# Two rotations between reciprocal and rescaling, the key tile and the index weights next, the last two index tiles behind them

## The chip, the cores and the metric

One core of a Trainium2 chip runs the whole program in one launch. The metric is the device time of one execution in microseconds, the median of three runs.

## What is computed

Four layers on x (512 tokens, width 1024, float32): two hybrid layers of the first kind (`a`), a final RMS norm, two of the second kind (`b`). What matters here is the head of each layer.

```python
# layer a: h = rmsnorm(x) * g ; z = h @ w_in
aq = rope_half(aq.reshape(B, S, 8, 64), pos)      # 8 query heads: tiles 0 to 3
ak = rope_half(ak.reshape(B, S, 2, 64), pos)      # 2 key heads: tile 4
ya = sliding_window_sink_attention(aq, ak, av, sinks) @ w_a
rq, rk = retention_rotation(...)                  # rotated inside attention
# layer b: proj = x @ w_in
aq, ak = partial_rope(aq), partial_rope(ak)       # tiles 0 to 7
iq = partial_rope(iq.reshape(B, S, 8, 64), pos)   # index queries: tiles 8 to 11
ik = partial_rope(ik)                             # index key, with the index weights: tile 12
score = sum_h w[t,h] * relu(iq[t,h] . ik[s])      # then the 128 largest per token are kept
```

## The kernel before

**Layout.** Everything is kept transposed: width on partitions, 512 tokens along the row, so a tile is 128x512. Products are made in float32 from a high and a low half: `split_products` (L490 to L492) issues three matmuls, w_hi x_hi, w_hi x_lo and w_lo x_hi. Weights come as 274 panels of 1 MB in one fixed stream. SyncE loads panel c (L312, L319, L324) when GpSimd has finished with panel c-2; ScalarE makes the high half (`hi`, L1137, two activations of 128x1024) and GpSimd the low half (L343, four subtractions of 128x512). A full 256-column panel is 48 matmuls for two tiles; the panel with tile 12 (104 columns) has 24.

**Order.** Each engine runs one list of instructions, written out by hand as one function per engine, with semaphores between them. `Steps.after(...)` puts waits ahead of the next instruction, `Steps.done(..., name)` gives its end a name in `marks`. On one engine nothing overtakes: an instruction that waits holds up all behind it. This is true of DMA issues on ScalarE's queue too: `const_dma` (L284) first waits until the constant load issued before it has landed.

```python
            if n_consts[0]:
                eng.wait_ge(const_loaded, 16 * n_consts[0])
            eng.dma_start(dst, src).then_inc(const_loaded, 16)
```

**Norm at the head of layer a.** The first two panels are multiplied with x g, not yet scaled by 1/rms. ScalarE splits x (L1400), squares it (L1161), VectorE adds the squares (L1764), TensorE sums them over partitions (L599), ScalarE takes the root (`token_root`, L1393), VectorE the reciprocal (`token_inverse`, L1801), and TensorE spreads it over partitions (L639) into PSUM bank 5, behind the second of the eight steps of panel 1. VectorE then rescales x tile by tile (L1835), ScalarE takes the high half (L1156, after TensorE has read the old one), VectorE the low half (L1742). From these panels 2 onward are multiplied. Behind this loop ScalarE splits panel 3 (`hi(panel + 3)`, at k = 5), and panel 2 directly behind the root. The final norm before the first `b` layer works in the same way, with panel 3 split at k = 0.

**Rotations.** `rope` on VectorE is four instructions: a shuffle (L1747, one input), two products with the rotation table (L1749, L1751) and a sum (L1753), each of the latter with two SBUF inputs. In layer `a` tiles 0 to 3 come from the unscaled panels, so each is then multiplied by the spread reciprocal (L2061). They are done in the order 0, 1, 2, 3, 4, behind the norm and the negated sinks (L2056). TensorE's first scores (L665) wait for `("roped", 4)` and for the values (`v_read`, L1459), and so does ScalarE's load of the next rotation table. VectorE's first step of attention is L1848.

**Head of layer b.** VectorE rotates tiles 8 to 12 in this order (tiles 8 and 9 come from the first index panel, 10 and 11 from the second, 12 from the third), reads the index weights (L2130, which waits for TensorE's transposes L977 of tile 12), does four small operations (L2134 to L2144) and goes into a loop over tiles 0 to 7: rotate, then `weigh` (L2156, L2158) the dot products that TensorE made behind that tile (`dots`, L987). `dots(i)` waits for tile 12, the index weights and, from i = 2, for ScalarE's read of dots i-2 (L1546), which waits for `weigh` to free its buffer. Behind the loop VectorE selects the largest (L2176, L2179) for two of three blocks and then begins attention (L1848).

**Start.** ScalarE issues the vector load, then the load of identity and ones, splits panel 0, splits x. Behind the squares it issues the load of the other constants (128x1540) and of the rotation table, and then goes on to the root.

## Time and profile before

| | |
|---|---|
| median of three runs | 3451.24 us (3449.07 to 3453.99) |
| profiled execution | 3451.36 us, its span 3449.6 us |
| mean granted TensorE clock | 0.993 of 2.4 GHz |
| TensorE busy | 3362.9 us, 97% |
| VectorE, ScalarE, GpSimd busy | 1600.6, 1429.1, 1460.3 us |

TensorE leaves little of the span unused, and the other three are each under half busy over the whole. Shares over the whole say nothing of the heads of the layers, though: these begin at 0, about 800, about 1600 and about 2520 us, each engine's list is followed there by its timeline, and what counts is whose last instruction TensorE waits for. A row of a timeline gives start, duration, engine, line, operation with output and input, count, and in brackets the idle time before it and what ended it. PEclk is the granted clock as a share of full speed: 1.00 is 2.4 GHz, 0.50 is 1.2 GHz.

### The profile page before, as it was taken

To read this page: it belongs to the slowest core of one execution; us is meant where nothing else is said; L and a number is where in the kernel's file an instruction comes from. 1 tells how busy PE (TensorE), PEld (TensorE's weight loads), DVE (VectorE), ACT (ScalarE), POOL (GpSimd) and SP (SyncE) were. 2 spreads that over 40 slices of the span, in tenths; PEclk is the share of its full clock that TensorE was granted. 3 is DMA by queue.
4 is the path that set the end of the run, shared out by engine and by line. 5 is a ranking of instruction groups with operands and counts; after the bars stand their busy time and mean duration, and the time that the engine had idled before them with its cause. 6 is when DMAs were issued, how large, how long until landed. Compare 5 with 4: busy or idle time off the path is not lost. (4 is left out here: it accounts for less than half of the span.)

```text
span 3449.6 us, 45699 instructions
## 1 busy us (share of the span) xinstructions
PE 3362.9 (97%) x16684; PEld 2762.7 (80%) x16684; DVE 1600.6 (46%) x2551; ACT 1429.1 (41%) x2082; POOL 1460.3 (42%) x1100
## 2 busy tenths in 40 slices
PE   7999999999999999998999999999999999999998
PEld 5788888887788888887768878888878788788886
DVE  6624232226624442225872346444488524364445
ACT  4644242224645342223364453433344634453333
POOL 4334444444333544444433335445534333444452
PEclk9999999999999999999999999999999999999999
DMA  3221222222222222222112222222312121222221
GB/s 136 73 79 70 98 97 98 97 98 97 71 79 74 99 97 98 97 97 98 65 61 74 74 80 95 86 97 97 110 62 86 50 80 68 87 84 98 97 97 61
DMA packets 43824, 298.65 MB, mean 87 GB/s; under 512 B 4816, under 2 KB 5456, under 8 KB 8592
## 3 DMA queue, kind: packets, MB, share of 16 engines
q1 hardware_dynamic: 41696, 291.52, 23.7%
q10 hardware_dynamic: 1968, 4.94, 0.4%
q8 instruction: 107, 1.75, 0.2%
q14 instruction: 53, 0.43, 0.0%
HBM read 294.34 MB, written 2.10 MB: 86 GB/s over the span
## 5 line engine op out<-in xcount | busy, mean ns | idle before, releaser
L343 POOL TENSOR_TENSOR w_lo<-w_raw,w_hi 128x512 fp32r<-128x512 f32 x1040 | 1379.6, 1359 | 1926.5 <-ACT w_hi L1137 1926.5
L490 PE MATMUL ps<-x_hi,w_hi 128*128 128x512 f32 x2576 | 1024.4, 398 | 27.0 <-POOL w_lo L343 20.9
L491 PE MATMUL ps<-x_lo,w_hi 128*128 128x512 f32 x2576 | 1006.1, 391 | 0.0
L492 PE MATMUL ps<-x_hi,w_lo 128*128 128x512 f32 x2576 | 1006.0, 391 | 0.0
L1137 ACT ACTIVATE w_hi<-w_raw 128x1024 fp32r<-128x1024 f32 x520 | 520.0, 1049 | 487.0 <-PE ps L492 432.2
L490 PEld LDWEIGHTS ps<-x_hi,w_hi 128*128 128x128 f32 x2576 | 485.4, 188 | 149.0 <-POOL w_lo L343 22.2
L492 PEld LDWEIGHTS ps<-x_hi,w_lo 128*128 128x128 f32 x2576 | 485.3, 188 | 103.1
L491 PEld LDWEIGHTS ps<-x_lo,w_hi 128*128 128x128 f32 x2576 | 485.9, 189 | 99.6 <-issue 2.4
L490 PE MATMUL ps<-y_hi,w_hi 128*128 128x512 f32 x1184 | 462.4, 391 | 4.3 <-POOL w_lo L343 2.1
L491 PE MATMUL ps<-y_lo,w_hi 128*128 128x512 f32 x1184 | 461.4, 390 | 0.0
L492 PE MATMUL ps<-y_hi,w_lo 128*128 128x512 f32 x1184 | 461.2, 389 | 0.0
L2011 DVE TENSOR_TENSOR x<-x,ps 128x512 f32<-128x512 f32 x272 | 182.4, 686 | 249.3 <-PE ps L492 249.1
L1970 DVE SCALAR_TENSOR_TENSOR arena<-ps,vec,arena 128x511 f32<-128x511 f32 (+1 forms) x176 | 131.5, 749 | 316.4 <-ACT arena L1327 306.2
L490 PEld LDWEIGHTS ps<-y_hi,w_hi 128*128 128x128 f32 x1184 | 222.5, 188 | 54.8 <-POOL w_lo L343 3.8
L492 PEld LDWEIGHTS ps<-y_hi,w_lo 128*128 128x128 f32 x1184 | 222.7, 188 | 46.4
L491 PEld LDWEIGHTS ps<-y_lo,w_hi 128*128 128x128 f32 x1184 | 222.7, 188 | 46.0
L1152 ACT ACTIVATE arena<-ps 128x512 f32<-128x512 f32 x160 | 95.7, 598 | 375.2 <-PE ps L492 327.4
L558 PE MATMUL ps<-w_hi,x_hi 128*128 128x256 f32 x768 | 221.9, 289 | 0.0
L559 PE MATMUL ps<-w_hi,x_lo 128*128 128x256 f32 x768 | 217.2, 283 | 0.0
L560 PE MATMUL ps<-w_lo,x_hi 128*128 128x256 f32 x768 | 217.2, 283 | 0.0
L1327 ACT ACTIVATE arena<-ps,vec 128x512 f32<-128x512 f32 x88 | 68.1, 779 | 275.7 <-PE ps L492 275.6
L1981 DVE SCALAR_TENSOR_TENSOR arena<-ps,tmp 128x512 f32<-128x512 f32 x64 | 44.1, 691 | 238.4 <-PE ps L492 224.8
(244 smaller groups left out, 3617.0 us busy)
## 6 DMA issues: line engine op xcount, KB each, us to landing
w_raw<-stream SPq DMA_DIRECT2D x274, 1024.0 KB, 4.8
x<-x_t SPq DMA_DIRECT2D x4, 512.0 KB, 7.5
rotary<-rot ACTq DMA_DIRECT2D x4, 512.0 KB, 3.6
y_t<-x SPq DMA_DIRECT2D x8, 256.0 KB, 2.0
ct<-consts ACTq DMA_DIRECT2D x2, 770.0 KB, 5.4
arena<-pos ACTq DMA_DIRECT2D x2, 256.0 KB, 2.6
vec<-vectors ACTq DMA_DIRECT2D x4, 116.0 KB, 2.1
ct<-consts ACTq DMA_DIRECT2D x1, 128.0 KB, 5.6
```

Of the source, the lines that this page charges most:

```text
L343: ins = nc.gpsimd.tensor_tensor(low(c)[:, o:o + S], RAW[:, c % 2, o:o + S], high(c)[:, o:o + S].bitcast(F32), ALU.subtract)
L490: pe.matmul(ps, wh, xh, start=(k == 0), stop=False)
L491: pe.matmul(ps, wh, xl, start=False, stop=False)
L492: return pe.matmul(ps, wl, xh, start=False, stop=last)
L558: pe.matmul(ps, xh, wh, start=(k == 0), stop=False)
L559: pe.matmul(ps, xl, wh, start=False, stop=False)
L560: mm = pe.matmul(ps, xh, wl, start=False, stop=(k == KD - 1))
L1137: act.activation(wh[:, o:o + 2 * S], RAW[:, s, o:o + 2 * S], ACT.Copy).then_inc(hi_ready, 1)
L1152: A.done(act.activation(dst, bank_of(*name), func, **kw), *(("read",) + name))
L1327: act.activation(AR[:, j, :], PS[:, j, :], ACT.Identity, scale=VEC[:, l % 2, bass.ds(tap, 1)], bias=VEC[:, l % 2, bass.ds(bias, 1)]).then_ ...
L1970: ins = dve.scalar_tensor_tensor(AR[:, j, tap:S], PS[:, j, 0:n], wv, AR[:, j, tap:S], ALU.mult, ALU.add)
L2011: dve.tensor_tensor(X[:, m, :], X[:, m, :], PS[:, 4 + m % 4, :], ALU.add).then_inc(down_added, 1)
```

## The change

Nothing is computed in another way; instructions change places and one is added.

- VectorE, layer `a`: the rotations of tiles 0 and 1 stand between the reciprocal and the rescaling (they wait for the sum over partitions too, whose input shares their scratch tile). Their factors follow the sinks, then tile 4, then tiles 2 and 3 with factor. Scores and ScalarE's table load wait for tile 3, now the last.
- VectorE, final norm: the rotations of tiles 8 and 9 of the first `b` layer stand between reciprocal and rescaling.
- VectorE, layer `b`: tile 12 next, then index weights and small operations, then tiles 10 and 11. TensorE's `dots(i)` waits for tile 8 + j as well.
- ScalarE, start: a copy of one column behind the vector load, so that the table load stands ahead of panel 0; the load of identity and ones behind panel 0's split; the rotation table's load ahead of panel 1's split, the other constants' load behind the root.

```diff
@@ -386,7 +386,7 @@
                 out.append(dict(nk=nk * P, q=AR[:, j, n * P:(n + 1) * P], k=AR[:, 4, k0 * P:(k0 + nk) * P],
                                 v=lambda kb, k0=k0: AR[:, 5, (k0 + kb) * P:(k0 + kb + 1) * P],
                                 mask=CT[:, 1796 - nk * P:1796], sink=2 * j,
-                                ready=[("a", l, "v_read"), ("a", l, "roped", 4)],
+                                ready=[("a", l, "v_read"), ("a", l, "roped", 3)],
                                 o=AR[:, 14 + j, n * P:(n + 1) * P]))
             return out
 
@@ -980,7 +980,7 @@
                 def dots(i):
 
                     b, j, bank = 1 + i // 4, i % 4, 4 + 2 * (i % 2)
-                    T.after((t, l, "dots_read", i - 2) if i >= 2 else (t, l, "roped", 12), (t, l, "iw_read"),
+                    T.after((t, l, "dots_read", i - 2) if i >= 2 else (t, l, "roped", 12), (t, l, "iw_read"), (t, l, "roped", 8 + j),
                             bank_reader[7], own=False)
                     for v in range(2):
                         h = slice(64 * v, 64 * v + 64)
@@ -1400,16 +1400,17 @@
                     A.done(act.activation(XH[:, k, :], X[:, k, :], ACT.Copy, scale=gain[:, k:k + 1]), t, l, "u_hi", k)
                     if (t, l) != ("a", 0):
                         run(squared)
+                if (t, l) == ("a", 0):
+                    const_dma(act, ROT[:, :, :], rot_in[0], ("rot", l, 0))
                 hi(panel + 1)
                 for _ in squared:
                     pass
-                if (t, l) == ("a", 0):
-                    const_dma(act, CT[:, 256:CW], consts_in[0, :, 256:CW], "consts_a")
-                    const_dma(act, ROT[:, :, :], rot_in[0], ("rot", l, 0))
                 warm_root()
                 for name, dst in first_tiles:
                     read(name, dst)
                 token_root(PS[:, 4, 0:S:P], (t, l, "n1_ms"), (t, l, "n1_root"))
+                if (t, l) == ("a", 0):
+                    const_dma(act, CT[:, 256:CW], consts_in[0, :, 256:CW], "consts_a")
                 hi(panel + 2)
                 for k in range(KD):
                     src = X[:, k, :] if to_x else TMP[:, k % 2, :]
@@ -1419,8 +1420,10 @@
                         hi(panel + 3)
 
             const_dma(act, VEC[:, 0, :], vec_in[0], "vec0")
+            A.after("eps")
+            A.done(act.activation(ST[:, 98:99], ST[:, 96:97], ACT.Copy))
+            hi(0)
             const_dma(act, CT[:, 0:256], consts_in[0, :, 0:256], "ident_ones")
-            hi(0)
             for l in range(DEPTH):
                 w, t = at_a(l), "a"
                 if l:
@@ -1459,7 +1462,7 @@
                 A.done(act.activation(AR[:, 5, :], PS[:, 6, :], ACT.Copy), t, l, "v_read")
                 if l == 0:
                     const_dma(act, VEC[:, 1, :], vec_in[1], "vec1")
-                A.after((t, l, "roped", 4))
+                A.after((t, l, "roped", 3))
                 const_dma(act, ROT[:, :, :], rot_in[1], ("rot", l, 1))
                 attention(pairs_a(l), l, t, filler_reads())
                 hi(w["wa"] + 1)
@@ -1814,9 +1817,11 @@
                 for _ in added:
                     pass
 
-            def norm(t, l, gain, to_x=False):
+            def norm(t, l, gain, first_ropes, to_x=False):
                 which = "n1"
                 token_inverse(t, l, which)
+                for _ in first_ropes:
+                    pass
 
                 def dst(k):
                     return X[:, k, :] if to_x else TMP[:, k % 2, :]
@@ -2050,15 +2055,24 @@
                 if l == 0:
                     for _ in stream_parts(t, l, VEC[:, 0, VA["g_mix"]:VA["g_mix"] + KD]):
                         pass
-                norm(t, l, VA["g_mix"])
+                def rope_a(j):
+                    rope(AR[:, j, :], SWAP_A, (t, l, "roped", j),
+                         [("read", t, l, "q", j), ("rot", l, 0), (t, l, "n1_ms")])
+
+                def factor_a(j):
+                    V.after()
+                    V.done(dve.tensor_tensor(AR[:, j, :], AR[:, j, :], PS[:, 5, :], ALU.mult), t, l, "roped", j)
+
+                norm(t, l, VA["g_mix"], (rope_a(j) for j in range(2)))
                 o = VA["sinks"]
                 V.after((t, l - 1, "negmax", 15) if l else None)
                 V.done(dve.tensor_scalar(ST[:, 16:24], VEC[:, l % 2, o:o + 8], -1.0, None, ALU.mult))
-                for j in range(5):
-                    rope(AR[:, j, :], SWAP_A, (t, l, "roped", j), [("read", t, l, "q", j), ("rot", l, 0)])
+                for j in range(2):
+                    factor_a(j)
+                for j in (4, 2, 3):
+                    rope_a(j)
                     if j < 4:
-                        V.after()
-                        V.done(dve.tensor_tensor(AR[:, j, :], AR[:, j, :], PS[:, 5, :], ALU.mult), t, l, "roped", j)
+                        factor_a(j)
 
                 def retention_ropes():
                     for j in range(8):
@@ -2114,17 +2128,18 @@
                 g = VA["g_mix"] if l + 1 < DEPTH else VB["g_final"]
                 ffn(l, t, FF1_GROUPS, 4, *bases(t, l),
                     stream_parts(*(("a", l + 1) if l + 1 < DEPTH else ("f", 0)), VEC[:, 1, g:g + KD]))
-            norm("f", 0, VB["g_final"], to_x=True)
+
+            def rope_b(l, j):
+                rope(AR[:, j, :], SWAP_B, ("b", l, "roped", j), [("read", "b", l, "q", j), ("b", l, "rot_tables")],
+                     YSCR[:, KD + 1, :])
+
+            norm("f", 0, VB["g_final"], (rope_b(0, j) for j in tiles_b(0)), to_x=True)
 
             for l in range(DEPTH):
                 t = "b"
                 V.after("vec2" if l == 0 else "vec3")
-                def rope_b(j):
-                    rope(AR[:, j, :], SWAP_B, (t, l, "roped", j), [("read", t, l, "q", j), (t, l, "rot_tables")],
-                         YSCR[:, KD + 1, :])
-
-                for j in range(8, 13):
-                    rope_b(j)
+                for j in (12,) if l == 0 else (8, 9, 12):
+                    rope_b(l, j)
                 iw = ST[:, 32:64].rearrange("p (n h) -> p n h", n=NB)
                 V.after((t, l, "iw"))
                 V.done(dve.tensor_scalar(iw, PS[:, 6, :].rearrange("p (n c) -> p n c", n=NB)[:, :, 96:104], 8 ** -0.5, None,
@@ -2142,6 +2157,8 @@
                 V.done(dve.memset(m0, 0.0))
                 V.after()
                 V.done(dve.memset(m0[0:64, 64:128], NEG), t, l, "mask", 0)
+                for j in (10, 11):
+                    rope_b(l, j)
 
                 def weigh(i):
 
@@ -2161,7 +2178,7 @@
                         V.done(dve.memset(sc[0:64, b * P + 64:(b + 1) * P], NEG))
 
                 for j in range(8):
-                    rope_b(j)
+                    rope_b(l, j)
                     for u in dots_behind(j):
                         weigh(u)
 
```

**ScalarE at the start**, difference of its list (minus before, plus changed):

```order
 L284 DMA vec<-vectors 128x232
+L1424 ACT_TABLE_LOAD
+L1424 ACTIVATE stats<-stats 128x1
+L1137 ACTIVATE w_hi<-w_raw 128x1024 x2
 L284 DMA ct<-consts 128x256
-L1137 ACT_TABLE_LOAD
-L1137 ACTIVATE w_hi<-w_raw 128x1024 x2
 L1400 ACTIVATE x_hi<-x,vec 128x512 x8
+L284 DMA rotary<-rot 128x1024
 L1137 ACTIVATE w_hi<-w_raw 128x1024 x2
```

The table load and panel 0's split moved ahead of the second constant load; the rotation table's load moved ahead of panel 1's split.

**VectorE at the norm of the first layer**, from the sums of squares on, before:

```order
L1801 RECIPROCAL stats<-stats 128x4
L1835 SCALAR_TENSOR_TENSOR tmp<-x,vec,ps 128x512 x2
L1742 TENSOR_TENSOR x_lo<-tmp,x_hi 128x512
L1835 SCALAR_TENSOR_TENSOR tmp<-x,vec,ps 128x512
L1742 TENSOR_TENSOR x_lo<-tmp,x_hi 128x512
```

and changed (lines have shifted: L1801 is now L1804, L1835 is L1840, L1742 is L1745, the rotation is L1750 to L1756):

```order
L1804 RECIPROCAL stats<-stats 128x4
L1750 STREAM_SHUFFLE tmp<-arena 128x512
L1752 TENSOR_TENSOR tmp<-tmp,rotary 128x512
L1754 TENSOR_TENSOR arena<-arena,rotary 128x512
L1756 TENSOR_TENSOR arena<-arena,tmp 128x512
L1750 STREAM_SHUFFLE tmp<-arena 128x512
L1752 TENSOR_TENSOR tmp<-tmp,rotary 128x512
L1754 TENSOR_TENSOR arena<-arena,rotary 128x512
L1756 TENSOR_TENSOR arena<-arena,tmp 128x512
L1840 SCALAR_TENSOR_TENSOR tmp<-x,vec,ps 128x512 x2
L1745 TENSOR_TENSOR x_lo<-tmp,x_hi 128x512
L1840 SCALAR_TENSOR_TENSOR tmp<-x,vec,ps 128x512
```

Eight instructions of two rotations now stand between the reciprocal and the first rescaling.

**VectorE at the head of the fourth layer**, from the last instruction of tile 12's rotation on, before:

```order
L1753 TENSOR_TENSOR arena<-arena,scratch 128x512
L2130 TENSOR_SCALAR stats<-ps 128x32
L2136 MEMSET arena 32x512
L2138 COPY arena<-arena 16x512
L2142 MEMSET arena 128x128
L2144 MEMSET arena 64x64
L1747 STREAM_SHUFFLE scratch<-arena 128x512
L1749 TENSOR_TENSOR scratch<-scratch,rotary 128x512
L1751 TENSOR_TENSOR arena<-arena,rotary 128x512
L1753 TENSOR_TENSOR arena<-arena,scratch 128x512
L2156 TENSOR_SCALAR arena<-tmp,stats 128x256
```

and changed (L2145 is the former L2130, L2151 to L2159 the small operations):

```order
L1756 TENSOR_TENSOR arena<-arena,scratch 128x512
L2145 TENSOR_SCALAR stats<-ps 128x32
L2151 MEMSET arena 32x512
L2153 COPY arena<-arena 16x512
L2157 MEMSET arena 128x128
L2159 MEMSET arena 64x64
L1750 STREAM_SHUFFLE scratch<-arena 128x512
L1752 TENSOR_TENSOR scratch<-scratch,rotary 128x512
L1754 TENSOR_TENSOR arena<-arena,rotary 128x512
L1756 TENSOR_TENSOR arena<-arena,scratch 128x512
L1750 STREAM_SHUFFLE scratch<-arena 128x512
```

Before, one rotation (tile 0) stood between the small operations and the first weighing L2156. Now these four rows come three times, for tiles 10, 11 and 0, before the weighing; ahead of the piece, the two rotations of 10 and 11 are gone. The third layer has the same order here, with one more small operation.

## Rows read from the trace of the kernel before

**Rows 1.** Waits of TensorE over the whole span: us in total, times, longest us.
```profile
PE ps L490 <- POOL w_lo L343: 23.0, 9, 15.0
PE ps L987 <- DVE stats L2130: 14.3, 2, 11.7
PE ps L665 <- DVE arena L1753: 11.3, 2, 6.0
...
PE ps L639 <- DVE stats L1801: 3.8, 1, 3.8
```

**Rows 2.** Timeline of ScalarE from the start: start us, us, engine, line, op, idle before.
```profile
6.26 0.33 ACTq L284 DMA_DIRECT2D ct<-consts  x1
6.63 1.28 ACT L1137 ACT_TABLE_LOAD   x1 [6.63 <-DMA vec<-vectors]
7.92 2.00 ACT L1137 ACTIVATE w_hi<-w_raw 128x1024 fp32r<-128x1024 f32 x2
...
32.37 1.28 ACT L1388 ACT_TABLE_LOAD   x1 [5.15 <-DMA ct<-consts]
...
35.33 0.26 ACT L1393 ACTIVATE stats<-ps,stats 128x4 f32<-128x4 f32 x1
```

**Rows 3.** Line L312, the load of the first weight panel.
```profile
DMA to landing us min/median/max: 5.3/5.3/5.3
```

**Rows 4.** Timeline of VectorE, first layer, 37 to 75 us.
```profile
37.76 1.41 DVE L1835 SCALAR_TENSOR_TENSOR tmp<-x,vec,ps 128x512 f32<-128x512 f32 x2 [1.96 <-PE ps L639]
...
51.94 1.14 DVE L2056 TENSOR_SCALAR stats<-vec 128x8 f32<-128x8 f32 x1
...
73.47 0.69 DVE L1753 TENSOR_TENSOR arena<-arena,tmp 128x512 f32<-128x512 f32 x1
```

**Rows 5.** Four windows, all engines: window, length, busy per engine, PEclk, DMA share, GB/s.
```profile
74.31:84.19 9.88, 9.07 (x33) 6.89 (x33) 2.32 (x13) 5.57 (x13) 4.13 (x4) 0.69 0.18 55
860.14:869.66 9.52, 8.71 (x33) 6.65 (x33) 2.32 (x13) 5.57 (x13) 3.76 (x4) 0.72 0.18 57
2563.07:2569.82 6.75, 6.75 (x33) 5.11 (x33) 5.80 (x13) 1.20 (x2) 0.77 (x1) 1.00 0.41 155
2657.14:2664.44 7.30, 6.70 (x34) 5.10 (x33) 3.99 (x15) 6.93 (x13) 2.05 (x2) 1.00 0.02 8
```

**Rows 6.** Timelines of VectorE and GpSimd, second layer, 819 to 825 us.
```profile
823.75 1.41 DVE L1835 SCALAR_TENSOR_TENSOR tmp<-x,vec,ps 128x512 f32<-128x512 f32 x2 [4.45 <-PE ps L639]
...
819.94 5.04 POOL L343 TENSOR_TENSOR w_lo<-w_raw,w_hi 128x512 fp32r<-128x512 f32 x4 [0.20 <-ACT w_hi L1137]
```

**Rows 7.** Timeline of VectorE, fourth layer, GpSimd splitting a panel from 2539.95 on.
```profile
2539.95 1.84 DVE L1751 TENSOR_TENSOR arena<-arena,rotary 128x512 f32<-128x512 f32 x1
2541.83 1.67 DVE L1753 TENSOR_TENSOR arena<-arena,scratch 128x512 f32<-128x512 f32 x1
...
2543.63 0.75 DVE L1747 STREAM_SHUFFLE scratch<-arena 128x512 f32<-128x512 f32 x1
```

**Rows 8.** Third layer: ScalarE and VectorE timelines, one window over all engines.
```profile
1608.98 1.41 DVE L1835 SCALAR_TENSOR_TENSOR x<-x,vec,ps 128x512 f32<-128x512 f32 x2 [4.65 <-PE ps L639]
...
1626.81 0.59 ACT L1560 ACTIVATE arena<-ps 64x512 f32<-64x512 f32 x1
...
1643.56:1699.53 55.97, 55.97 (x261) 41.64 (x260) 46.76 (x66) 21.07 (x28) 22.26 (x15) 0.97 0.15 57
...
1738.90 0.29 DVE L1848 CUSTOM_DVE_ANT_0 tmp<-arena,ps 128x128 f32<-128x128 f32 x1 [0.66 <-PE ps L665]
```

**Rows 9.** The same places of the fourth layer.
```profile
2555.88 0.59 ACT L1560 ACTIVATE arena<-ps 64x512 f32<-64x512 f32 x1
...
2562.82 0.19 DVE L2130 TENSOR_SCALAR stats<-ps 128x32 f32<-128x32 f32 x1
...
2564.69:2618.33 53.64, 53.64 (x258) 39.98 (x257) 46.85 (x66) 20.89 (x27) 22.32 (x15) 1.00 0.22 79
...
2657.68 0.29 DVE L1848 CUSTOM_DVE_ANT_0 tmp<-arena,ps 128x128 f32<-128x128 f32 x1 [0.30 <-PE ps L665]
```


## The prediction, made before the changed kernel was run

> **What bounds the kernel now.** I read the page first, then TensorE's waits, then the timelines of the engines around the four longest of them. TensorE is busy for 3362.9 of 3449.6 us, so only its waits and its slow-clock stretches can be won. In the list of its waits [rows 1] three places depend on the order that the change touches. The start: 15.0 us until the first weight panel is split. The beginning of dot products in the two `b` layers, which waits for VectorE's L2130: 11.7 us in the first, 2.6 in the second. The beginning of attention in the two `a` layers, which waits for the last rotation (L1753): 11.3 us, 6.0 of them in the second and so 5.3 in the first. A fourth, 3.8 us at L639, is TensorE waiting for the reciprocal of the first norm.
>
> **How each place works.** Start [rows 2, 3]: ScalarE's queue stands until 6.26 us for the small vector load, because the next DMA issue waits for it; then the 1.28 us table load follows, and the first split begins at 7.92, though its panel had landed at 0.75 + 5.3 = 6.05. Norm [rows 2]: ScalarE idles 5.15 us before its second table load, behind the 770 KB constant load for which the issue of the rotation table waits; that stands in front of the root at 35.33. Attention: VectorE does the norm's eight tiles, then five rotations one behind the other, and ends at 73.47 + 0.69 = 74.16 [rows 4]; TensorE had arrived at 74.31 - 5.31 = 69.0. Between reciprocal and rescaling VectorE stands idle for 1.96 us in the first layer, 4.45 in the second, 4.65 in the third [rows 4, 6, 8]. That idle time is what the change fills.
>
> **Start and first layer.** The table load moves ahead of the panel's landing, so the split begins at about 6.1 instead of 7.92: 1.8 us. The sums behind it hang on x too, and I carry 1.5. ScalarE then reaches its last square 1.5 earlier and no longer loses the 5.15: the reciprocal comes 6.6 us earlier, at 29.0. Now VectorE does two rotations before rescaling. A rotation is one shuffle of 0.75 and three operations of 0.69, with some 0.2 of gaps: 3.0, so 6.0 for two. But GpSimd splits panel 2 in just these microseconds (its split starts about 1.1 after the root). What that costs: operations with two SBUF inputs took 1.84 and 1.67 beside a split instead of 0.69, the shuffle stayed at 0.75 [rows 7]. Over a whole split: five rotations and four factors undisturbed are 5 x 3.0 + 4 x 0.82 = 18.4; measured from 53.08 to 74.16 they took 21.1, so one split costs them 2.7 [rows 4]. Bounds for two rotations: 0 if the two miss each other; 5.0 if all four GpSimd operations of 1.26 (5.04 / 4, [rows 6]) block VectorE in full. I take 2.9, near the measured 2.7, with the two slowest of rows 7 in mind.
>
> The Trainium skill speaks against the change here: its page SBUF — State Buffer (section Who interferes with whom) says that a VectorE instruction with two SBUF inputs contends with a GpSimd instruction that reads SBUF and that whoever comes second fully blocks. The trace agrees for the operations of rows 7. By that rule alone, with VectorE always second, each pair costs 5.0 instead of 2.9; that case is a rival below.
>
> Rescaling then begins at 29.2 + 6.0 + 2.9 = 38.1, no earlier than before (37.76). Its loop and the negated sinks took 37.76 to 53.08, 15.3, of it 1.3 beside the split of panel 2, which is over by now: done at 52.1. Behind it come two factors (1.6), the key tile (3.0), two rotations with factor (7.7) and one more split (2.7): 67.1 against 74.16, so attention begins 7.0 earlier. Is VectorE still the last? TensorE would arrive 1.5 + 3.8 earlier than 69.0, less what it now waits for late halves of x, and the read of the transposed values comes 0.9 behind: 65 to 66. Yes; a wait of some 2.5 us is left. The large constant load, now behind the root, lands near 35 and is first needed past 60; it costs nothing.
>
> **The clock.** After the waits of 5.3 and 6.0 the same 33 products took 9.88 and 9.52 us at a mean clock of 0.69 and 0.72; the like stretch at full clock took 7.30, and after a wait of 2.6 us the clock stayed at 1.00 [rows 5]. The waits left here are about 2.5 and 2.8, so I take the clock as kept: 2.4 and 2.0 us (of differences of 2.6 and 2.2). The other bound is 0. First layer: 7.0 + 2.4 = 9.4.
>
> **Second layer.** The reciprocal ends at 823.75 - 4.45 = 819.3; two rotations beside the split of panel 2 [rows 6] end at 819.3 + 8.9 = 828.2, so rescaling comes 4.5 later than before, and what VectorE does from there shrinks by two rotations (6.0), and by the 0.5 it idled in the loop: 2.0 earlier at attention. TensorE's panels 2 and 3 are held up by about 1 us, under the same wait. With the clock 4.0. Bounds: 0 with the lock at its worst and the clock lost, 6 without any blocking.
>
> **Third layer.** Here rescaling is 8.9 behind the reciprocal instead of 4.65: 4.3 later. The 104-column panel has only 24 products, so TensorE feels all of it, and so does the copy of tile 12 that ended at 1627.4 [rows 8] and now ends at 1631.7. One rotation beside a split (5.2) and the scaling of the weights put the dot products at 1637.2 instead of 1641.7: TensorE gains 4.5. But rotations 10 and 11 now stand behind: with 2.4 of small operations (one of them beside the split) and 6.2 for the two, the loop over tiles 0 to 7 begins at 1645.8, 2.2 later than before. VectorE idles 55.97 - 46.76 = 9.2 us in that loop [rows 8]; its 66 instructions have gaps of 0.04 to 0.13 [rows 7], 4.4 together, so 4.8 can be made up. It reaches attention 2.6 earlier, and had 0.66 to spare: TensorE gains 3.3 there, not 4.5 and not the slow clock.
>
> **Fourth layer.** No rotation moves ahead of the norm, and tile 12 is there only at 2555.88 + 0.59 = 2556.5. In the 8 us before, VectorE did rotations 10 and 11; now it stands idle. The dot products begin at most 0.8 earlier, the loop 5.6 later (1.87 after L2130 as before, plus 6.2, less 0.6 to 0.8). Its idle time is 53.64 - 46.85 = 6.8, less 4.4 of gaps: 2.4 to make up [rows 9]. VectorE comes 3.2 late to attention, had 0.30 to spare, so TensorE loses 2.8. Bounds: 0 if the idle time takes all, 5.3 if none.
>
> **Sum.** 9.4 + 4.0 + 3.3 - 2.8 = 13.9. The profiled execution took 3451.4 us (span 3449.6 and 1.8 around it), the median of the three runs is 3451.24, so both are the same base: 3437.5. A difference under 0.2% (6.9 us) can't be told from none.
>
> **The rivals.**
> - *No blocking*: the two rotations fit between GpSimd's operations. Then 3 us come on top in the first, 2 in the second, 3 in the third layer: 3429.5. Against it: rows 7, and GpSimd starts less than 1 us behind the reciprocal.
> - *The lock at its worst*, with the clock lost too: 2.1 less at three places gives 3443.8, one clock drop 3446. For it: waits of 2.5 to 2.8 lie close to the longest that kept the clock.
> - *The change doesn't do what it says*: VectorE's chain, merely reordered, comes out at the same length everywhere; only start and norm pay, 6.6, less 2.8: 3447.6.
> - *Slower*: VectorE's backlog in the `b` layers. ScalarE reads the dot products into two buffers that VectorE's weighing frees, and behind these reads in its queue stand the splits of the next panels. If the late loop never catches up, TensorE takes the whole delay: 4.3 (2.2 + 2.1) in the third and 5.6 in the fourth layer, and with nothing won in the `a` layers (their kv panel starved by the late rescaling) that is 3461. It decides from the point where weighing a tile takes longer than the 7 us that TensorE gives it per tile. Against it: the idle time in the loop, and that the reads had 1 us and more in hand.
>
> **Chances.** Forecast 0.60 (own range 3433 to 3442), no blocking 0.16, lock at its worst 0.16, nothing from reordering 0.05, slower 0.03. Of the third a quarter lies above 3444.3, where "same" begins. So faster 0.60 + 0.16 + 0.12 = 0.88, same 0.04 + 0.05 = 0.09, slower 0.03. The range takes in the forecast's bounds and most of the two cases beside it: 3429 to 3445.
>
> **What would show it.** First split near 6.1, first product near 13.1, reciprocal near 29, spread without wait. Rotations of tiles 0 and 1 in the three norms with operations of 1.7 instead of 0.69, about 8.9 for both. Waits at L665 for a rotation of 2 to 3 us each, with PEclk at 1.0 behind them. In the third layer a wait of about 3 before the dot products and a new one of 1 to 3 at the second scores; in the fourth 8 us of idle VectorE before tile 12 and a wait of 3 at the second scores. Wrong would be: rotations in 6.1, full-length waits at attention, or a fourth layer that loses nothing.

## The result, and the profile after

| | before | changed |
|---|---|---|
| median | 3451.22 us (20 runs, 3449.07 to 3453.99) | 3456.37 us (20 runs, 3455.47 to 3457.14) |
| span of the profiled execution | 3449.6 us | 3454.4 us |
| mean granted clock | 0.993 | 0.992 |

The ratio is 1.0015, with a 95% interval from 1.0008 to 1.0022: 5 us slower, where 14 us faster was predicted. That is under the 0.2% that the prediction called "same", yet the interval excludes no change, and the range is missed by 11 us.

TensorE's waits in the changed kernel, against [rows 1] (us in total, times, longest):

```profile
PE ps L490 <- POOL w_lo L343: 22.3, 10, 13.6
PE ps L665 <- DVE stats L1853: 15.5, 4, 7.0
PE ps L490 <- DVE x_lo L1745: 6.4, 8, 1.3
PE ps L665 <- DVE arena L2064: 5.8, 2, 3.4
...
PE ps L987 <- DVE stats L2145: 3.9, 2, 2.7
```

The waits that the change was to shorten did shrink: ahead of the dot products 14.3 to 3.9 us, ahead of the `a` attentions 11.3 to 5.8 us, the one at L639 is gone. But the wait for the maxima grew from 2.8 us before (four waits, the longest 0.8, at L1848) to 15.5 us (L1853), and x halves now come late (6.4 us instead of 0.8).

First, second and third scores (L665) in TensorE's timeline of the changed kernel, one block for each layer (start us, us, engine, line, op, idle before):

```profile
68.98 0.77 PE L665 MATMUL ps<-arena 64*128 64x128 f32 x4 [3.39 <-DVE arena L2064]
70.55 0.89 PE L665 MATMUL ps<-arena 64*128 64x128 f32 x4 [0.81 <-DVE stats L1853]
79.22 0.49 PE L665 MATMUL ps<-arena 64*128 64x128 f32 x4
...
852.36 0.58 PE L665 MATMUL ps<-arena 64*128 64x128 f32 x4 [2.44 <-DVE arena L2064]
...
861.51 0.49 PE L665 MATMUL ps<-arena 64*128 64x128 f32 x4
...
1725.43 0.49 PE L665 MATMUL ps<-arena 64*128 64x128 f32 x4
1732.88 0.87 PE L665 MATMUL ps<-arena 64*128 64x128 f32 x4 [6.96 <-DVE stats L1853]
1741.50 0.49 PE L665 MATMUL ps<-arena 64*128 64x128 f32 x4
...
2652.72 0.49 PE L665 MATMUL ps<-arena 64*128 64x128 f32 x4
2660.15 0.87 PE L665 MATMUL ps<-arena 64*128 64x128 f32 x4 [6.94 <-DVE stats L1853]
2667.72 0.49 PE L665 MATMUL ps<-arena 64*128 64x128 f32 x4
```

In both `b` layers TensorE now reaches the attention early and stands 7 us before the second scores, which wait for VectorE's first maxima, which stand behind the loop over tiles 0 to 7 and the selection of the 128 largest. The start of the third scores is a good milestone in each layer, since the waits that the change touches all lie ahead of it. Taken from each trace, minus the time before (84.19, 869.66, 1745.65, 2664.44, span 3449.6); "layer" is counted from one of these points to the next:

| third scores, us against before | layer 1 | layer 2 | layer 3 | layer 4 | span |
|---|---|---|---|---|---|
| changed | -5.0 | -8.2 | -4.2 | +3.3 | +4.8 |
| e1, `a` layers and start only | -5.2 | -8.4 | -8.1 | -8.4 | -8.3 |
| e2, `b` layers only | -0.5 | -0.7 | +3.2 | +12.3 | +12.3 |
| e3, old order in both `b` | -5.9 | -9.0 | -9.2 | -9.3 | -9.3 |
| e4, old order in layer 4 alone | -5.7 | -9.0 | -5.0 | -5.6 | -5.6 |
| e5, start only | -6.7 | -6.7 | -6.8 | -7.0 | -7.0 |
| e6, e3 with the rotations behind the rescaling | -5.7 | -5.6 | -5.6 | -5.7 | -5.8 |
| e8, dot products held back | -5.3 | -8.5 | -7.5 | -1.7 | -1.8 |
| e9, tile 10 back ahead of tile 12 | -5.7 | -7.5 | -5.7 | +0.4 | +0.4 |
| e10, wait in `b` filled | -6.3 | -8.2 | -6.7 | -0.7 | -0.8 |
| e7, wait in `a` filled | -7.9 | -12.8 | -12.8 | -13.0 | -13.1 |

The table shows single executions, and these are not the medians: that of e3 is 1.1 us faster than e3's median, that of e4 1.2 and that of e2 1.0, that of e6 0.5 slower and that of e8 1.0. Seven of the kernels have the same instructions up to the first point (changed, e1, e3, e4, e8, e9, e10) and stand there between -5.0 and -6.3, so a difference of 1 us between two rows at one point can be chance.

So the changed kernel wins 5.0 and 3.2 us in the `a` layers, loses 4.0 and 7.4 in the `b` layers, and 1.5 behind the last of these points. One place where VectorE stood idle in each `b` layer, in its timeline of the changed kernel:

```profile
1623.74 0.01 DVE L1750 LOAD_MASK_SELECT scratch<-arena  x1 [4.45 <-ACT arena L1563]
...
2552.21 0.01 DVE L1750 LOAD_MASK_SELECT scratch<-arena  x1 [7.92 <-ACT arena L1563]
```

These are the starts of tile 12's rotation in layers 3 and 4, waiting for ScalarE's read of it. In the fourth layer before, the rotations of tiles 10 and 11 filled this time; now it is empty, and they follow behind. And four windows, the two loops over tiles 0 to 7 and the stretches from second to third scores (window, length, busy per engine PE, PEld, DVE, ACT, POOL, then PEclk, DMA share, GB/s):

```profile
1637.90:1693.47 55.57, 55.03 (x290) 42.65 (x289) 51.18 (x66) 22.02 (x29) 25.95 (x17) 1.00 0.17 59
2565.17:2620.75 55.58, 54.61 (x288) 42.29 (x287) 51.19 (x66) 22.34 (x28) 26.34 (x17) 1.00 0.17 59
1732.88:1741.50 8.62, 8.62 (x29) 6.61 (x29) 3.77 (x10) 5.13 (x11) 5.13 (x4) 0.68 0.01 3
2660.15:2667.72 7.57, 7.57 (x28) 5.83 (x28) 3.78 (x10) 5.14 (x11) 4.08 (x4) 0.79 0.00 0
```

In the loops the same 66 VectorE instructions are busy for 51.2 us instead of 46.8 [rows 8, 9], with 17 of GpSimd's operations beside them instead of 15. GpSimd's splits met VectorE's work before too, but other parts of it: in the loop of layer 3 the 24 two-input operations of the rotations went from 19.5 to 27.2 us and the 21 weighings from 20.1 to 16.7. In the last two windows the clock is down; the same stretch at full clock takes 6.2 us (e10 below).

### The profile page after: what moved, and what is told of

Same layout as the page of the kernel before. It is cut to its first block and busy times, and to the rows that moved or that the text cites. A ratio compares the mean times of both kernels' runs of the same rounds, so it can differ in the third digit from the quotient of the medians.

```text
span 3454.4 us, 45710 instructions
## 1 busy us (share of the span) xinstructions
PE 3368.7 (98%) x16684; PEld 2764.2 (80%) x16684; DVE 1615.0 (47%) x2551; ACT 1428.0 (41%) x2083; POOL 1466.7 (42%) x1100
## 5 line engine op out<-in xcount | busy, mean ns | idle before, releaser
L490 PEld LDWEIGHTS ps<-y_hi,w_hi 128*128 128x128 f32 x1184 | 222.6, 188 | 54.6 <-POOL w_lo L343 3.7
L1152 ACT ACTIVATE arena<-ps 128x512 f32<-128x512 f32 x160 | 95.6, 597 | 331.3 <-PE ps L492 283.0
```

The lines of the kernel that those rows point to most:

```text
L490: pe.matmul(ps, wh, xh, start=(k == 0), stop=False)
L1152: A.done(act.activation(dst, bank_of(*name), func, **kw), *(("read",) + name))
```

## The experiments

Each was compared with the kernel before on the same chip; medians of that were 3451.1 to 3451.6 us. I had three accounts of the loss: T1, VectorE's order around tile 12; T2 and T3, that the earlier arrival of all work or the rotations ahead of the final norm cost it; C, the clock behind the new waits. A fourth, P, came with e8: VectorE's loop got longer because TensorE, running ahead, drew more of GpSimd's splits into it.

**e1, e2: the change in two halves.** e1 keeps start and `a` layers and does tiles 8 to 12 in the old order behind the final norm; e2 is the complement.

```diff
-            norm("f", 0, VB["g_final"], (rope_b(0, j) for j in tiles_b(0)), to_x=True)
+            norm("f", 0, VB["g_final"], (), to_x=True)
-                for j in (12,) if l == 0 else (8, 9, 12):
+                for j in range(8, 13):
                     rope_b(l, j)
...
-                for j in (10, 11):
-                    rope_b(l, j)
```

> The change without its part on the `b` layers: start and both `a` layers as changed; tiles 8 to 12 in the old order behind the final norm. Theory T1 (in the `b` layers VectorE reaches the attention late, because it waits for tile 12 with tiles 10 and 11 still to do): the gains of the `a` layers that the trace of the changed kernel shows, 5.0 and 3.2 us, stay whole: 3451.2 - 8.2 = 3443.0 us. Theory T2 (what the `a` layers gain is lost in `b` whatever the order there, because all of TensorE's and GpSimd's work arrives 8 us earlier against a VectorE that cannot follow): 3449 us or more, with a wait of TensorE for the first maxima of some 7 us in layer 3.

> The change's part on the `b` layers alone: start and `a` layers as before; tiles 8 and 9 ahead of the final norm, tile 12 and the index weights ahead of tiles 10 and 11. T1: both losses that the trace of the changed kernel shows, 4.1 us in layer 3 and 7.5 us in layer 4, stand alone: 3451.2 + 11.6 = 3462.8 us, with TensorE waiting some 7 us for maxima (L1853) in each of the two. T2: 3451 to 3454 us.

e1: 3443.03 us, ratio 0.9977 (0.9967 to 0.9987). e2: 3464.72 us, ratio 1.0040 (1.0026 to 1.0054). The change is, to half a microsecond, the sum of one half that wins 8.1 us and one that loses 13.6, which is 2 us more than the 11.6 that T1 expected of it. T2 falls: with TensorE 8 us ahead but the old order, nothing is lost. TensorE's timeline of e2, second scores of the two `b` layers:

```profile
1740.39 0.87 PE L665 MATMUL ps<-arena 64*128 64x128 f32 x4 [6.95 <-DVE stats L1850]
...
2667.86 0.87 PE L665 MATMUL ps<-arena 64*128 64x128 f32 x4 [7.30 <-DVE stats L1850]
```

**e3, e4: which part of the `b` half.** e3 has tiles 10 and 11 ahead of tile 12 again, but leaves 8 and 9 ahead of the final norm; e4 has the old order in the last layer alone.

```diff
-                for j in (12,) if l == 0 else (8, 9, 12):
+                for j in (10, 11, 12) if l == 0 else range(8, 13):      # e3
+                for j in (12,) if l == 0 else range(8, 13):             # e4
...
-                for j in (10, 11):                                      # e3: gone, with the line below it
+                for j in (10, 11) if l == 0 else ():                    # e4
```

> The changed kernel with tiles 10 and 11 ahead of tile 12 again in both `b` layers (8 and 9 stay ahead of the final norm). T1: layer 4 is as before (gain of 7.5 us on the changed kernel); in layer 3 the rotations ahead of the norm fill time in which VectorE waited, and tile 12 is the only one behind the reads: at least the 4.1 us back and perhaps 1 to 2 us more: 3441 to 3444 us. T3 (the two rotations ahead of the final norm, beside GpSimd's split, are what costs VectorE its time in layer 3): layer 3 keeps 2 to 4 us of its loss, 3445 to 3447 us.

> The changed kernel with the old order 8, 9, 10, 11, 12 in the last layer only. T1: the 7.5 us of that layer come back: 3448.9 us; the wait of 6.9 us for maxima (L1853) stays in layer 3 and is gone in layer 4. If the wait in layer 4 follows from TensorE's earlier arrival and not from VectorE's order, less than 2 us come back: over 3454 us.

e3: 3443.12 us, ratio 0.9975 (0.9966 to 0.9985). e4: 3447.05 us, ratio 0.9987 (0.9978 to 0.9996). T3 falls: with the rotations of 8 and 9 ahead of the final norm the time is e1's to 0.1 us, so they neither cost nor bring anything. The traces show why. Ahead of the rescaling the pair takes 9.0 us beside GpSimd's split, behind it e1's first rotation takes 3.1. So in e3 the rescaling begins 4.4 us later behind the reciprocal (9.3 instead of 4.9), and so do TensorE's products; VectorE then waits 1.9 us for tile 10, and the 6.1 us that it no longer has to do are used up. VectorE in e3:

```profile
1595.09 0.18 DVE L1804 RECIPROCAL stats<-stats 128x4 f32<-128x4 f32 x1 [4.02 <-ACT stats L1393]
...
1604.39 1.40 DVE L1840 SCALAR_TENSOR_TENSOR x<-x,vec,ps 128x512 f32<-128x512 f32 x2
...
1620.34 0.01 DVE L1750 LOAD_MASK_SELECT scratch<-arena  x1 [1.90 <-ACT arena L1152]
```

T1 stands. e4 gives back 9.3 us, more than the 7.5 expected: its trace has 8.0 of it in layer 4, and the 1.5 us behind that layer are not lost (the table's last two columns). TensorE's timeline, second scores of layer 4, in e4:

```profile
2652.67 0.56 PE L665 MATMUL ps<-arena 64*128 64x128 f32 x4 [0.60 <-DVE stats L1853]
```

**e9: tile 10 back ahead of tile 12, tile 11 behind it.**

```diff
-                for j in (12,) if l == 0 else (8, 9, 12):
+                for j in (10, 12) if l == 0 else (8, 9, 10, 12):
...
-                for j in (10, 11):
+                for j in (11,):
```

> The changed kernel with tile 10 ahead of tile 12 and only tile 11 behind it, in both `b` layers. T1 (VectorE's idle time before tile 12, 4.5 us in layer 3 and 7.9 us in layer 4, is what the loss is made of): tile 10 takes 3 to 5 us of it, so layer 3 gets its 4.1 us back, layer 4 some 4 of its 7.5 us: 3456.4 - 8 = 3448 us, 3446 to 3450. If what counts is only that tiles stand behind the index weights, half of the total of 11.6 us comes back in each layer: 3450.5 us or more.

3451.61 us, ratio 1.0002 (0.9993 to 1.0011): 4.8 us back, where T1 said 8, and its alternative "3450.5 or more" fits the total. Its traces say why the total misleads. VectorE's idle time before tile 12 fell to 2.80 us in layer 4, and the waits before the second scores fell too, but the clock was lost behind a wait of 4.4 or 5.6 us as behind one of 7: the stretches that follow took 8.5 and 8.7 us, where the changed kernel has 8.6 and 7.6. TensorE's timeline and two windows of e9:

```profile
1731.45 0.87 PE L665 MATMUL ps<-arena 64*128 64x128 f32 x4 [4.39 <-DVE stats L1853]
...
2656.17 0.87 PE L665 MATMUL ps<-arena 64*128 64x128 f32 x4 [5.62 <-DVE stats L1853]
```
```profile
1731.45:1739.98 8.53, 8.53 (x28) 6.51 (x28) 3.77 (x10) 5.14 (x11) 5.03 (x4) 0.69 0.01 3
2656.17:2664.86 8.69, 8.69 (x29) 6.63 (x29) 3.77 (x10) 5.14 (x11) 5.19 (x4) 0.68 0.00 0
```

From layer 3's third to layer 4's second scores took 912.6 us before, 918.7 in the changed kernel and 916.2 here: tile 10 alone returns 2.5 of VectorE's 6.1 us in layer 4, though it fills 5.1 of the 7.9 us of idle time. T1 in the form "the idle time is what the loss is made of" is thus half the account; e8 shows another part.

**e10: the wait in the `b` layers filled.** Products that nothing reads keep TensorE busy in the new wait.

```diff
                 scores(0)
+                if t == "b":
+                    T.after(bank_reader[6], own=False)
+                    for i in range(30):
+                        pe.matmul(PS[:, 6, :], XH[:, 0, 0:P], XH[:, 0, :], start=True, stop=True)
                 scores(1)
```

> The changed kernel with 30 products that nothing reads (128x128 by 128x512, 6.8 us, into bank 6) between first and second scores of the `b` layers, where TensorE waits 7.0 and 6.9 us. Theory C: the stretches from second to third scores, 8.6 us at a clock of 0.68 in layer 3 and 7.6 us at 0.79 in layer 4, go back to 6.2 and 6.2 at full clock; of them 1.9 and 0.8 us more than in the kernel before come back for certain, 3.8 at most: 3452.6 to 3453.7 us. If the clock has no part, 3456.4 us.

3450.83 us, ratio 1.0000 (0.9991 to 1.0009), 5.5 us less than the changed kernel; the second scores begin when they did (1732.76), only the clock differs. Windows of e10 from second to third scores:

```profile
1732.76:1738.94 6.18, 6.18 (x30) 4.78 (x29) 3.79 (x10) 5.12 (x11) 3.01 (x3) 1.00 0.02 4
2657.61:2663.75 6.14, 6.14 (x29) 4.78 (x29) 3.78 (x10) 5.13 (x11) 2.97 (x3) 1.00 0.01 3
```

8.62 and 7.57 us became 6.18 and 6.14, 3.8 us together, the most that was expected. The other 1.5 is the one that the changed kernel loses after the last third scores: its windows show two dips of the clock there. The kernel before has the first alone, and so e10 has the second alone (0.91 in 2940:2960). Changed kernel, then before:

```profile
2750.00:2770.00 20.00, 20.00 (x96) 15.53 (x95) 4.20 (x7) 11.21 (x18) 4.97 (x4) 0.91 0.17 63
2940.00:2960.00 20.00, 18.21 (x73) 14.26 (x72) 9.82 (x8) 8.80 (x11) 5.47 (x4) 0.92 0.27 100
```
```profile
2750.00:2770.00 20.00, 20.00 (x83) 15.02 (x82) 5.52 (x8) 11.67 (x18) 5.21 (x5) 0.91 0.16 52
2940.00:2960.00 20.00, 18.21 (x79) 14.39 (x78) 9.62 (x7) 9.85 (x12) 8.36 (x7) 1.00 0.14 53
```

That the filling is what avoided the second dip is not shown: which of the two places dips differs from kernel to kernel.

**e8: the dot products held back.** VectorE's list as changed, TensorE's first dot products wait for tile 10.

```diff
-                    ... (t, l, "iw_read"), (t, l, "roped", 8 + j),
+                    ... (t, l, "iw_read"), (t, l, "roped", 8 + j if i else 10),
```

> The changed kernel, in whose `b` layers TensorE's first dot products also wait for tile 10 (some 3 to 5 us later than in the changed kernel); VectorE's list is untouched. Theory P (VectorE's loop over tiles 0 to 7 takes longer since TensorE runs ahead and draws one more of GpSimd's splits into it: 17 GpSimd operations in the fourth layer's loop instead of 15): with TensorE held back the loop takes 1 to 2 us less in each layer and the wait for maxima shrinks by more: 3452.5 to 3455 us. If only VectorE's order counts and the collisions stay, the total does not move, since TensorE has 7 us in hand: 3456.4 us.

3448.65 us, ratio 0.9991 (0.9982 to 1.0000): a wait added to the busiest engine made the kernel 7.7 us faster, far more than the 1.4 to 3.9 expected. The loops of e8, in the same windows as above:

```profile
1637.42:1692.08 54.66, 54.66 (x258) 40.70 (x258) 46.80 (x68) 20.44 (x26) 22.22 (x15) 0.98 0.16 58
2561.79:2616.63 54.84, 54.84 (x258) 40.88 (x257) 46.75 (x67) 20.45 (x26) 22.25 (x15) 0.97 0.16 58
```

VectorE's busy time is back at 46.8 us and GpSimd's operations at 15, as theory P has it: the 4.4 us more were collisions, and they came with TensorE running ahead. Yet the loops shrank by only 0.9 and 0.7 us, because VectorE now waits 4.0 and 4.3 us in them for tiles from TensorE (by way of ScalarE's reads, L1152), and the second scores came only 0.6 and 0.3 us sooner after the third scores of the layer before. The rest of the gain is behind the second scores: the wait there is 0.61 us instead of 7, and the stretches to the third scores take 6.2 us each at full clock, 3.8 us less together; one of the two later dips is missing too (1.4 us).

The clock is not saved altogether, though. TensorE now waits ahead of the dot products (8.5 and 5.8 us; 11.7 and 2.6 before the change), and the clock falls there, in good part ahead of the two windows above. The first 10 us from the dot products on, in layers 3 and 4 of e8, then the same of the changed kernel, whose waits there were 2.7 and 1.2 us:

```profile
1634.53:1644.53 10.00, 10.00 (x37) 7.26 (x38) 7.64 (x16) 1.92 (x4) 0.00 (x0) 0.75 0.06 23
2558.69:2568.69 10.00, 10.00 (x36) 7.25 (x36) 7.44 (x14) 1.65 (x3) 0.00 (x0) 0.71 0.19 78
```
```profile
1628.97:1638.97 10.00, 10.00 (x41) 7.28 (x41) 9.03 (x18) 1.79 (x3) 1.98 (x2) 0.83 0.31 107
2557.43:2567.43 10.00, 10.00 (x47) 7.59 (x48) 9.02 (x19) 1.79 (x3) 2.20 (x2) 1.00 0.29 105
```

An estimate from these means and lengths: e8 loses some 2.5 and 2.9 us there, the changed kernel 1.7 and 0. So e8 has one fall of the clock in each layer where the changed kernel has two in layer 3 and one in layer 4. By the table it gains 3.0 us in layer 3, 1.6 in layer 4 and 1.4 behind; how layer 4's part divides between waits, clock and loop is not shown.

**e5, e6: the `a` half in parts.** e5 is the kernel before with the four edits on ScalarE at the start. e6 is e3 with the rotations of tiles 0 and 1 behind the rescaling.

```diff
-                norm(t, l, VA["g_mix"], (rope_a(j) for j in range(2)))
+                norm(t, l, VA["g_mix"], ())
...
                 for j in range(2):
+                    rope_a(j)
                     factor_a(j)
```

> The kernel before with the start's edits on ScalarE alone (warm copy, first split ahead of the small transfer, the constants and the rotation tables issued elsewhere). Theory S (the order of ScalarE's transfers is what brought the first reciprocal from 35.6 to 29.3): reciprocal at about 29, scores of the first attention 4 to 6 us earlier than 74.3, total 3445 to 3447 us. Theory R (only the 1.4 us of the first product come from the start, the rest from the rotations ahead of the rescaling): 3449.8 us, reciprocal near 34.

> The kernel of e3_b_old_order (3443.1 us) with the rotations of tiles 0 and 1 behind the rescaling in both `a` layers. Theory G (the two rotations ahead fill time in which VectorE waits for the reciprocal's spread, 4.5 us per layer): the rescaling starts some 7 us earlier, but the rotations follow it, and the scores come 2 to 3 us later per layer: 3447 to 3449 us. Theory L (the rotations ahead, at 1.66 us an operation beside GpSimd's split, give back what they fill, and make TensorE wait for x halves): 3442 to 3444 us.

e5: 3444.93 us, ratio 0.9981 (0.9972 to 0.9990): the start alone brings 6.2 of the half's 8.1 us. e6: 3445.12 us, ratio 0.9984 (0.9975 to 0.9993), 2.0 us above e3, between the two theories. VectorE and TensorE in e5, first layer:

```profile
28.74 0.18 DVE L1804 RECIPROCAL stats<-stats 128x4 f32<-128x4 f32 x1 [2.47 <-ACT stats L1393]
...
31.72 1.40 DVE L1838 SCALAR_TENSOR_TENSOR tmp<-x,vec,ps 128x512 f32<-128x512 f32 x2 [2.81 <-PE ps L639]
```
```profile
67.62 0.89 PE L665 MATMUL ps<-arena 64*128 64x128 f32 x4 [5.54 <-DVE arena L1756]
```

The table above shows where: in layer 2, with the rotations ahead, 3.2 us are won (e1, e3) and without them nothing (e5, e6). That this is more than the 2.0 us between the medians of e3 and e6 is partly a matter of the executions profiled, which are 3.5 us apart. In layer 1 the reciprocal stands 38.9 us ahead of the first scores in e5, 39.3 in e6 and 39.7 in all kernels that have the rotations ahead: there the new order costs 0.8 us, 0.4 of it by the rotations ahead (e3 against e6) and 0.4 by the key tile ahead of tiles 2 and 3 (e6 against e5, which differ in this layer by little else).

**e7, e11, e12: the waits of the `a` layers filled.** e7 is e3 with filling ahead of the first scores. e11 has the rotations ahead in layer 2 alone (in layer 1 the order is e6's, with the key tile ahead of tiles 2 and 3), the `b` layers as in e1, and 23 products in layer 1; e12 is e11 with 28.

```diff
+                if t == "a":
+                    T.after(bank_reader[4], own=False)
+                    for i in range(14 - 4 * l):        # e11: 10 if l else 23; e12: 10 if l else 28
+                        pe.matmul(PS[:, 4, :], XH[:, 0, 0:P], XH[:, 0, :], start=True, stop=True)
                 scores(0)
```

> The kernel of e3_b_old_order with products that nothing reads (14 in layer 1, 10 in layer 2, 128x128 by 128x512, into the bank that the first scores then overwrite) put into TensorE's wait ahead of the first scores (3.4 and 2.4 us in e3_b_old_order's trace). Theory C (the granted clock of 0.68 and 0.81 between the first and the third scores follows that wait): clock 0.95 or more in these stretches, which shrink from 10.0 and 9.1 us to some 7.3 each, total 3438.5 to 3440 us. If the clock falls without it, or the stretches hang on ScalarE and GpSimd instead: 3443 us and the same stretches.

> The start's edits, the rotations ahead of the rescaling in layer 2 alone, the old order everywhere else, and fill products in TensorE's wait of both `a` layers (23 and 10). From the traces: reciprocal to first scores took 38.9 us with layer 1 in the old order (e5_start_only) and 39.7 with the rotations ahead (e3_b_old_order); in layer 2 41.0 and 38.5. So layer 1 should gain 0.8 us on e7_fill_wait, layer 2 nothing: 3437.5 us. If the placement of GpSimd's splits eats it, 3438.3 or a little over.

> The kernel of e11_best (3440.0 us) with 28 instead of 23 fill products in layer 1, where its trace shows 1.3 us of waiting left ahead of the first scores and, behind it, 9.2 us from second to third scores against 6.2 in e7_fill_wait. Theory C (that remaining wait, short as it is, cost the clock): the stretch goes back to 6.2 us and the total to 3437.0 us (3436.5 to 3438). If the clock falls for another reason there: 3440.0 us.

e7: 3438.32 us, ratio 0.9964 (0.9950 to 0.9977). e11: 3440.04 us, 0.9968 (0.9955 to 0.9980). e12: 3438.32 us, 0.9964 (0.9951 to 0.9978). Windows from first to third scores of layers 1 and 2 in e7, and of layer 1 in e11 and in e12:

```profile
68.66:76.27 7.61, 6.80 (x33) 5.24 (x33) 2.32 (x13) 5.57 (x13) 2.38 (x2) 1.00 0.22 69
849.29:856.87 7.58, 6.77 (x32) 5.23 (x33) 2.32 (x13) 5.57 (x13) 2.35 (x2) 1.00 0.22 69
```
```profile
68.19:78.77 10.58, 9.77 (x32) 7.43 (x32) 2.32 (x13) 5.56 (x13) 5.00 (x4) 0.68 0.16 50
```
```profile
68.23:75.74 7.51, 6.69 (x33) 5.15 (x32) 2.32 (x13) 5.56 (x13) 2.44 (x2) 1.00 0.25 70
```

Theory C holds for each: without the wait the clock stays, and the stretch shrinks from 10.0 and 9.1 us (e3) to 7.6 and 7.6. In e11 a wait of 1.32 us was left, and with the 0.81 us before the second scores the clock fell to 0.68; five more products took it away, and the stretch was 7.5. The total followed by 1.7 us only, not by 3.0. e11's reckoned 0.8 us for layer 1 was wrong by half: I took it from e5, but the order there is e6's, and from reciprocal to first scores e11 takes 39.35 us, e6 39.32. So 0.4 us were to be had, and the clock took them; in e12 the 28 products run right up to the first scores, at 39.5. e12 reached e7's time but not the 3437.0 expected. Both, at 13 us under the kernel before, are the fastest of the series.

## Why the prediction was wrong

The terms, by the milestones (before minus changed; the stretch from first to third scores holds the clock's part):

| term | predicted | measured |
|---|---|---|
| layer 1, first scores | 7.0 | 5.3 |
| layer 1, clock | 2.4 | -0.4 |
| layer 2, first scores | 2.0 | 2.8 |
| layer 2, clock | 2.0 | 0.4 |
| layer 3 | 3.3 | -4.0 |
| layer 4 | -2.8 | -7.4 |
| behind it | 0 | -1.5 |
| sum | 13.9 | -4.8 |

- **Start: right.** Reciprocal predicted at 29.0, measured at 29.25; first split 6.57 (its panel landed 0.5 later), first product 13.60 instead of 14.95. e5 shows this step to be worth 6.2 us by itself: the rival in which the change does nothing else set it at 6.6.
- **Rotations beside the split: right in size.** 8.9 predicted for the pair; 9.0, 8.9 and 9.0 measured in the three norms, from the first shuffle to the rescaling. In layer 1 of the changed kernel VectorE's timeline shows operations of 1.66 us:

```profile
31.11 1.66 DVE L1754 TENSOR_TENSOR arena<-arena,rotary 128x512 f32<-128x512 f32 x1
32.81 1.66 DVE L1756 TENSOR_TENSOR arena<-arena,tmp 128x512 f32<-128x512 f32 x1
...
38.52 1.40 DVE L1840 SCALAR_TENSOR_TENSOR tmp<-x,vec,ps 128x512 f32<-128x512 f32 x2
...
49.12 3.43 DVE L1745 TENSOR_TENSOR x_lo<-tmp,x_hi 128x512 fp32r<-128x512 f32 x2
```

- **Layer 1, the sum "15.3, of it 1.3 beside the split of panel 2, which is over by now": wrong by 1.2.** Rescaling and sinks took 38.52 to 53.73, still 15.2. The split of panel 3 now lies on the end of it (3.43 for two operations, last row). What followed took 15.1 for the predicted 15.0. Together with rescaling beginning 0.4 late and 0.1 more behind it that is most of the 1.9 by which the first scores came late (68.98 for 67.1). TensorE arrived at 65.6, as predicted (65 to 66); by these figures 1.1 to 2.1 of waiting was to be expected and not "some 2.5", and 3.4 came. And the reordering is not what won in this layer: it costs 0.8 (e5 against e3).
- **The clock, "so I take the clock as kept": wrong, 4.4 of the 18.7 us.** Waits of 3.4 and 2.4 us were left, and behind them the clock was 0.67 and 0.81. e7 shows that these waits cause it: 4.0 us in the two stretches, 4.8 in the total. That a wait of 2.6 us ahead of the dot products had kept the clock [rows 5] was one row at another place; I used the loss of the clock for the other bound alone. And even at that place it isn't a rule: in layer 4 of e1 a wait of 2.54 us left a mean of 0.83 over the next 10 us, in layer 4 of e3 one of 2.56 us left 1.00.
- **Layers 3 and 4, "so 4.8 can be made up" and "2.4 to make up": the main failure.** That the dot products begin sooner was right for layer 3 (4.5 us predicted, 4.6 measured), and so was that VectorE enters the loop late: 2.2 predicted for layer 3, 2.5 measured; 5.6 and 4.6 for layer 4. But I took the idle time less the gaps in the loop as reserve, which sets the packed loop at 46.8 + 4.4 = 51.2 us. The loop shrank by 0.4 us in layer 3 (55.97 to 55.57) and grew by 1.9 in layer 4 (53.64 to 55.58). Packed tightly, the same instructions were busy for 51.2 instead of 46.8 us, because more of GpSimd's operations ran beside them and met the rotations' operations with two SBUF inputs, which took 1.66 us instead of 0.69 there. These 4.4 us are the whole difference between the 51.2 of the sum and the 55.6 measured. I had priced this on the two rotations and not on the loop. The Trainium skill, page SBUF — State Buffer, section Who interferes with whom, names the contention of such a VectorE operation with a GpSimd instruction that reads SBUF. Whether a packed loop without it can be had is not shown: e8 has the busy time of 46.8 but waits for TensorE instead. So against the third scores of the layer before, the second scores come 1.6 us later in layer 3 and 6.1 in layer 4, where I had 3.3 earlier and 2.8 later.
- **A cost that had no term at all: the clock behind the new wait.** I foresaw the wait (1 to 3 us) and gave it nothing. It cost 2.4 and 1.4 us; a later dip, 1.5 more. Together with VectorE's 7.6 that is 12.9, against the 13.6 of e2. (e2's own trace, 12.3 us behind the one before, has 3.9 in layer 3, 9.2 in layer 4 and nothing behind, so the agreement is partly chance.)
- **The rival that came nearest had a chance of 0.03.** VectorE's backlog in the `b` layers, decided "where weighing a tile takes longer than the 7 us that TensorE gives it": the loop's eight tiles took 55.6 us, 6.95 each, without a gap. VectorE was at that point, with no reserve beyond it. Its path was another, though: I had TensorE held up by late splits behind ScalarE's reads, and TensorE was busy for 55.0 and 54.6 of the loops' 55.6 us and waited only behind the loop, at the second scores, for 1.6 and 6.1 us of delay instead of 4.3 and 5.6. I held the loop's idle time against this rival, the same reading that failed in the sum; its other half, nothing won in the `a` layers, was wrong: 8.2 us were won there.

What stays open: why the new order costs 0.8 us in layer 1; why GpSimd's splits fall on the rotations once the loop is packed; why the later dip of the clock comes in some kernels and not in others; and what length or kind of wait costs the clock.

## What to carry to other kernels

Idle time inside a loop is no reserve when the busy time itself depends on how the work of another engine falls into it: count on the busy time of the packed loop, not of the loose one (here 4.4 us more on 46.8). Before an operation is moved ahead of others, look when its input arrives: here tile 12's did 4.5 to 8 us after VectorE was free, and the two tiles that had covered this time were put behind it. Where TensorE bounds the kernel and arrives early at a wait, the wait can cost more than its length through the clock: to fill the waits with unused products was worth 4.8 us (e7) and 5.5 (e10), and to hold TensorE back earlier 7.7 (e8), there with fewer collisions as well.

## What the runs showed of the hardware

- A wait of 1.32 us and one of 0.81 us close behind it took the granted clock to a mean of 0.68 of 2.4 GHz over 10.6 us (e11); 0.22 and 0.81 us at the same place left it at 1.00 (e7). Waits of 2.4 to 7 us before the scores cost it each time, 1.4 to 2.7 us of time, and its price did not grow with the wait's length (0.69 behind 4.4 us, 0.68 behind 7.0). e8's waits of 8.5 and 5.8 us ahead of the dot products left 0.75 and 0.71 over the next 10 us, the first 2.9 and 3.1 of them at 0.50, that is 1.2 GHz.
- The length of a wait alone did not decide: at the same place, ahead of the dot products of layer 4, 2.56 us left the clock at 1.00 over the next 10 us (before, e3) and 2.54 us left 0.83 (e1); ahead of those of layer 3, 2.71 us left 0.83 (changed).
- VectorE's busy time for 66 identical instructions was 46.8 or 51.2 us, by where 15 to 17 GpSimd subtractions fell; these took 1.60 us each in the packed loop (6.38 for four) and 1.26 alone [rows 6].
- A VectorE operation with two SBUF inputs took 0.69 us alone and 1.66 beside GpSimd's subtractions, a shuffle with one input 0.72 to 0.76 either way. A pair of the two took 1.66 to 1.70 us, less than 0.69 + 1.26 = 1.95: they hindered each other but did not take turns for their whole lengths.
